# Last expert's rows in an array of their own, the other gathers beside its products, second bias added to the rows

## What is computed

```
logits = xt @ router_w + router_b
top_logit, top_idx = lax.top_k(logits, 4)          # of 32 experts
top_gate = softmax(top_logit)
for each expert e and each of its tokens:
    hid = xb @ w1[e] + b1[e]                       # 1024 -> 2048
    glu = minimum(hid[:, :1024], 7); lin = clip(hid[:, 1024:], -7, 7)
    act = glu * sigmoid(1.702 * glu) * (lin + 1)
    y   = (act @ w2[e] + b2[e]) * gate             # 1024 -> 1024
out[token] = sum of the token's four rows y
x = x + gate2 * out
```

## Time and profile before

| | |
|---|---|
| median of three runs | 2637.34 us (2634.68 to 2642.07) |
| profiled execution | 2637.1 us, span 2635.1 us, mean granted clock of TensorE 0.969 |
| PE busy | 2499.3 us (95%) |
| DVE, ACT, POOL busy | 39%, 15%, 7% |
| expert loop | about 629 to 1656 us of the span |
| end of the pass | about 1656 to 1707 us of the span |
| the chain that ended last, by engine | PE 92%, DVE 3%, ACT 2%, DMA 2%, POOL 1% |

### The profile page before, as it was taken

The page is one execution under the profiler, slowest core; times in us unless marked ns, Lnnn a source line. Parts: engine busy times, 40 slices in busy tenths (PEclk is TensorE's granted clock), DMA queues, the critical chain, the costliest instruction groups (busy, mean ns, idle before and its releaser), DMA issues.

```text
span 2635.1 us, 49056 instructions
## 1 busy us (share of the span) xinstructions
PE 2499.3 (95%) x20546; PEld 1392.9 (53%) x20546; DVE 1017.1 (39%) x2008; ACT 405.9 (15%) x797; POOL 195.1 (7%) x256
## 2 busy tenths in 40 slices
PE   5999989796999999999999999699999998999999
PEld 2444787653344433333344434345556544888888
DVE  5563655414333333333333333523145222455551
ACT  2411134412000000000000000101234201111100
POOL 0000000000111111111111111400000000000000
PEclk9999999887999999999999999799999999999999
DMA  7432000106999999999999999740200112222221
GB/s 275 156 128 96 2 3 1 67 0 248 413 422 422 421 422 422 421 422 422 422 422 422 422 422 384 253 164 33 96 33 33 32 32 64 64 96 64 88 66 54
DMA packets 143742, 555.43 MB, mean 211 GB/s; under 512 B 15760, under 2 KB 51632, under 8 KB 94240
## 3 DMA queue, kind: packets, MB, share of 16 engines
q1 hardware_dynamic: 127088, 515.22, 49.2%
q0 software_dynamic: 13984, 36.49, 3.8%
q10 hardware_dynamic: 2576, 2.36, 0.3%
HBM read 537.25 MB, written 16.78 MB: 210 GB/s over the span
## 4 chain that ended last, share of the span: by engine, by line
PE 92%; DVE 3%; ACT 2%; DMA 2%; issue 1%; POOL 1%; SPq 0%; POOLq 0%; DVEq 0%; ACTq 0%
PE psum L2501 25%; PE psum L2090 20%; PE psum L2517 13%; PE psum L2787 10%; PE psum L2816 5%; PE psum L2250 2%; PE psum L2706 2%; PE psum L2422 2%; PE psum L2683 1%; DMA ring<-in_ada_w 1%; PE psum L2364 1%; PE psum L2661 1%; PE psum L2390 1%; PE psum L2671 1%; PE psum L2078 1%
## 5 line engine op out<-in xcount | busy, mean ns | idle before, releaser
L2501 PE MATMUL psum<-ring,arena 128*32 128x512 f32 x6144 | 667.8, 594 | 10.2 <-DVE arena L1688 6.8
L2501 PEld LDWEIGHTS psum<-ring,arena 128*32 128x32 f32 x6144 | 196.8, 110 | 453.0 <-issue 452.3
L2090 PE MATMUL psum<-hT,ring 128*128 128x512 f32 x752 | 340.6, 610 | 3.5 <-ACT hT L833 3.5
L2517 PE MATMUL psum<-ring,arena 128*32 128x256 f32 x6144 | 338.3, 379 | 2.2 <-DVE arena L1722 2.1
L2517 PEld LDWEIGHTS psum<-ring,arena 128*32 128x32 f32 x6144 | 201.2, 110 | 146.5 <-issue 21.9
L2090 PEld LDWEIGHTS psum<-hT,ring 128*128 128x128 f32 x752 | 144.9, 196 | 182.2 <-issue 180.3
L1688 DVE STREAM_TRANSPOSE arena<-arena 128x768 f32<-128x768 f32 x33 | 32.3, 979 | 512.6 <-PE psum L2501 512.6
L764 POOL DMA_INDIRECT arena<-h_rows,small x102 | 99.9, 980 | 1294.8 <-issue 680.7
L2787 PE MATMUL psum<-ring 128*128 128x256 f32 x704 | 159.1, 379 | 0.5 <-ACT arena L819 0.5
L1017 ACT ACTIVATE arena<-arena 128x768 f32<-128x768 f32 x32 | 27.0, 843 | 823.3 <-DVE arena L1708 823.3
L2787 PEld LDWEIGHTS psum<-ring 128*128 128x128 f32 x704 | 133.7, 190 | 19.0 <-ACT arena L819 0.9
(11 more groups left out here) (393 smaller groups left out, 2553.3 us busy)
## 6 DMA issues: line engine op xcount, KB each, us to landing
ring<-in_exp_w SPq DMA_DIRECT2D x384, 1024.0 KB, 15.8
ring<-in_w_in SPq DMA_DIRECT2D x15, 2048.0 KB, 8.3
ring<-in_ada_w SPq DMA_DIRECT2D x12, 2048.0 KB, 7.8
ring<-in_w_ffn_in SPq DMA_DIRECT2D x22, 1024.0 KB, 7.7
expert_rows<-arena POOLq DMA_DIRECT2D x128, 96.0 KB, 6.0
ring<-in_w_ffn_out SPq DMA_DIRECT2D x8, 1408.0 KB, 6.8
ring<-in_w_out SPq DMA_DIRECT2D x2, 2048.0 KB, 7.9
ring<-in_w_o SPq DMA_DIRECT2D x2, 2048.0 KB, 8.5
```

What stands on the lines that cost most here:

```text
L2090: ins = mm(dst, l, r, start=(i == 0), stop=(i == len(parts) - 1))
L2501: ins = mm(bank[s][q * SG:(q + 1) * SG, :], XG[:, k, s * SG:(s + 1) * SG], w[:, q], start=(k == 0), stop=(k == KD - 1))
L2517: ins = mm(bank[3 + s // 2][q * SG:(q + 1) * SG, (s % 2) * 256:(s % 2 + 1) * 256], aT2k[:, s, k // 2, k % 2, :], w2_slot(k)[:, q * 256:(q ...
```

## The change

- `expert_rows` holds 31 experts; the rows of expert 31 (`LATE`) go to an HBM array of their own, `late_rows`.
- The loop has 29 rounds; two more are written out after it for PE and DVE, without number_slots and gathers for experts that do not exist (before, the loop ran these for experts 32 and 33).
- POOL stores expert 30, then issues the gathers of token tiles 0 and 1 (`fetch`), sends expert 31's rows, and issues tile 2 (after tile 0 is summed), tile 3, and after tile 2 is summed four gathers from `late_rows`, one per tile.
- The row index of each choice is clipped to the 31 experts and its gate is zeroed where the choice is expert 31 (two more small DVE steps); the gate of the late rows is taken from `GATE`.
- PE adds the four sums, then the four late tiles, so 8 rounds of 16 matmuls in place of 4.
- b2 is loaded per expert by ACT (`load_b2`, four DMAs of 1 KB), spread together with b1, and added where Y is copied out of PSUM. The load of all b2, the transposes of the gates, `GATE_T` and the L2538 products are gone.

```diff
-    keys += [("pos", t) for t in range(NT)] + [("cnt",), ("gateT",)]
+    keys += [("pos", t) for t in range(NT)] + [("cnt",)]
...
-        YR = [A(i, 2) for i in (14, 16, 18, 20, 0, 2, 4, 6, 8, 10, 12, 22, 24, 30, 14, 16)]
+        yr_room = [A(14, 2), A(16, 2), A(18, 2), A(20, 2), A(24, 2), A(30, 2), hflat[:, 4 * T:6 * T], hflat[:, 6 * T:8 * T]]
+        YR = yr_room + yr_room[1:4] + [A(0, 2), A(2, 2), A(4, 2), A(6, 2), A(8, 2)]
+        TOTAL = YR[::TOP_K]
+        YR_LATE = [yr_room[5], yr_room[6], yr_room[7], yr_room[2]]
...
-            sp.wait_ge(lin_ready, 1)
-            sp.dma_start(B2, a["exp_b2"][0]).then_inc(moe_in, 16)
...
+            def fetch(t):
+                for i in range(t * TOP_K, t * TOP_K + TOP_K):
+                    pool.indirect_dma_start(YR[i], None, y_d, ...choice_row[:, i:i + 1]...).then_inc(yr_in[t], 16)
...
-                with pool.Fori(0, EXPERTS - 1) as e:
+                with pool.Fori(0, EXPERTS - 3) as e:
                     gather(j, e + 3)
                     store(j, e)
-                store(j, EXPERTS - 1)
+                store(j, EXPERTS - 3)
+                store(j, EXPERTS - 2)
                 pool.wait_ge(rows_ready, j + 1)
                 pool.sem_inc(pool_turn, 1)
-                for i in range(NT * TOP_K):
...
+                fetch(0)
+                fetch(1)
+                send(j, LATE, y_late.rearrange("(s i) n -> s i n", s=GROUPS))
+                pool.wait_ge(choice_chain, summed(j, TOP_K))
+                pool.wait_ge(gx_sb, j * TURNS + (EXPERTS + 1))
+                fetch(2)
+                pool.wait_ge(aT_sb, j * EXPERTS + (EXPERTS + 1))
+                pool.wait_ge(w1_free, (j * EXPERTS + EXPERTS) * (QT4 * KD) + QT4 * KD)
+                fetch(3)
+                sent(j, LATE)
+                pool.wait_ge(choice_chain, summed(j, 3 * TOP_K))
+                for t in range(NT):
+                    pool.indirect_dma_start(YR_LATE[t], None, y_late, ...late_row[:, t:t + 1]...).then_inc(yr_last[t], 16)
...
+            def load_b2(e):
+                for q in range(QT4):
+                    act.dma_start(BIAS_ROWS[q * SG:q * SG + 1, 512:BIAS_N], a["exp_b2"][0][...]).then_inc(bias_in, 16)
...
-                dve.tensor_copy(Y, psum[:, 3 * T:3 * T + GROUPS * 256]...)
+                dve.tensor_tensor(Y, psum[:, 3 * T:3 * T + GROUPS * 256]..., B2[:, None, :].to_broadcast([P, GROUPS, 256]), ALU.add)
...
+                bias_arrived(j, EXPERTS - 1)
+                dve.tensor_copy(late_row, late_at).then_inc(choice_chain, 1)
+                spread_bias()
+                activations(j, LATE)
+                take_rows(j, LATE - 1)
+                turn_activations(j, LATE)
+                dve.wait_ge(bias_in, (j * EXPERTS + EXPERTS) * (32 * QT4))
+                dve.tensor_tensor(late_gate, late_gate, GATE[:, :, LATE], ALU.mult)
+                dve.stream_shuffle(BIAS_ALL, BIAS_ROWS, [0] * SG).then_inc(choice_chain, 1)
+                take_rows(j, LATE)
+                for t in range(NT):
+                    sum_rows(t)
+                for t in range(NT):
+                    dve.wait_ge(yr_last[t], j * 16 + 16)
+                    dve.tensor_scalar(YR_LATE[t], YR_LATE[t], late_gate[:, t:t + 1], None, ALU.mult).then_inc(sum_ready, 1)
...
-                for m in range(KD):
-                    mm(bank[m][:, :], B2[:, m * P:(m + 1) * P], GATE_T, start=True, stop=True)
+                for t in range(NT):
+                    pe.wait_ge(choice_chain, summed(j, (t + 1) * TOP_K))
+                    for m in range(KD):
+                        mm(bank[m][:, t * P:(t + 1) * P], TOTAL[t][:, m * P:(m + 1) * P], ident, start=(t == 0), stop=False, ...)
                 for t in range(NT):
                     pe.wait_ge(sum_ready, j * NT + (t + 1))
                     for m in range(KD):
-                        ins = mm(bank[m][:, t * P:(t + 1) * P], total[:, m * P:(m + 1) * P], ident, start=False, stop=True, ...)
+                        ins = mm(bank[m][:, t * P:(t + 1) * P], YR_LATE[t][:, m * P:(m + 1) * P], ident, start=False, stop=True, ...)
```

More of the change, by code:

```diff
@@ L334, in program @@
             "rows_ready", "mix_mm", "sum_ready", "choice_chain", "passed"))
-        yr_in = [sem(f"yr_in{t}") for t in range(NT - 1)]
-        yr_last = [sem(f"yr_last{r}") for r in range(TOP_K)]
+        yr_in = [sem(f"yr_in{t}") for t in range(NT)]
+        yr_last = [sem(f"yr_last{t}") for t in range(NT)]
         square2 = A(0, KD).rearrange("p (k t) -> p k t", k=KD)
@@ L461, in program @@
         choice_row = small[:, 16:32].bitcast(U32)
+        late_at = small[:, 96:100]
+        late_gate = small[:, 104:108]
+        late_row = small[:, 112:116].bitcast(U32)
         w1_slot = lambda k: ring[:, k * 2 * FF:(k + 1) * 2 * FF]
@@ L703, in _ @@
             w_o = a["w_o_2"][0].rearrange("(k p) n -> p k n", p=P)
-            for r in range(TOP_K):
-                sp.wait_ge(yr_last[r], passes * 16)
+            for t in range(NT):
+                sp.wait_ge(yr_last[t], passes * 16)
             for name, _ in chunks2:
@@ L767, in gather, with send @@
                 pool.sem_inc(idx_used, 1)
-            def store(j, e):
+            def send(j, e, rows):
                 pool.wait_ge(ye_sb, j * EXPERTS + (e + 2))
@@ L1769, in _ @@
                     look_up(j, e + 3)
[L1770 to L1775 removed]
+                bias_arrived(j, EXPERTS - 2)
+                turn_rows(j, EXPERTS - 1)
+                spread_bias()
+                activations(j, EXPERTS - 2)
+                take_rows(j, EXPERTS - 3)
+                turn_activations(j, EXPERTS - 2)
@@ L1782, in _ @@
                         else:
-                            dve.wait_ge(choice_chain, j * CHOICE_LINKS + (8 + t * (TOP_K - 1) + r))
-                            ins = dve.scalar_tensor_tensor(out=total, in0=YR[t * TOP_K + r], scalar=gate, in1=total,
-                                                           op0=ALU.mult, op1=ALU.add)
-                        ins.then_inc(choice_chain if r < TOP_K - 1 else sum_ready, 1)
+                            dve.wait_ge(choice_chain, summed(j, t * TOP_K + r))
```

112 lines of the change are left out of this document (62 added, 50 removed).

## The result

Over 20 runs each, the changed kernel took 2643.98 us and the kernel before 2636.75 us (medians): ratio 1.0023, 95% interval [1.0016, 1.003]. It is slower, by 7.2 us between the medians and 6.1 us by the ratio. That is less than the 0.3% that I had said a measurement can tell from no change, but the interval of these 20 runs leaves 1 out, so that limit was set too wide. (One run of 3057.83 us, at a granted clock of 0.82, is left out of the ratio.) The time forecast was 2640.1, in a range of 2633.0 to 2647.0. So the call and the range held, but the excess was put at +2.8 us and is more than twice that. And one of the prediction's own signs of being wrong has come: from the first w1 product (at 644.95, and 645.38 before) to the copy of expert 31 (1664.85, and 1655.49 before) it is 1019.9 us where it was 1010.1, 9.8 us longer, and the sign was set at 1 us.

A forecast was written before the change was run, and what follows sets the result against it. PE bounds the expert loop, with weight DMAs close behind; a chain of store, gathers and sums bounds the pass end. Last PE tile 1696.7 against 1693.9 gives +2.8 us: 2639.9, 2640.1 against the median; range 2633 to 2647.

The forecast's parts named there:

- 0.3% that I had said a measurement can tell from no change: Whole kernel: a measurement was said to tell about 0.3%, 7.9 us, from no change.
- one of the prediction's own signs of being wrong: Expert loop, first w1 product to copy of expert 31: prediction wrong if longer than before by over 1 us.
- b2 by expert: Expert loop: added small b2 loads make 1.9 us by the 30th round, below the cover, so they cost 0.
- 4.3 us of cover: Expert loop, last w1 loads: weights land in 24.7 us and may take up to 29.0 before PE waits.
- the rival of late weights: Expert loop: b2 packets make PE wait for w1 if above 0.14 us a round; 2647.2 us, chance 0.08.
- The rule that I had weighed and set aside: b2 loads in the loop: below 64 KB coalesce; read as a cost in latency, which nothing waits for.
- G = 1648.7: End of pass: first gather starts at 1648.7 us, 13.3 us before the old 1662.03.
- rows(31) "off the new path in any case": After the loop: expert 31's w2 product was said not to lie on the new path; loop exit taken as 0.
- late code: First unrolled product after the loop: 11.53 us against 10.54 inside, read as code arriving late, once; ends 0 and +1.0.
- Landing, three times in a row: End of pass: tile 0, tile 2 and late gathers each land in about 6.2 us, three waits where there were two.
- The rest of the path: End of pass, after G: tile 3 summed G + 36.7, late rows scaled G + 39.8, last PE tile ends G + 48.0.
- Edits at 0: Removed gate transposes and L2538 products, and leaving the loop two rounds earlier: each taken as 0.

The follow-up runs named there:

- e8: Changed kernel with each expert's b2 in one load of four rows instead of four 1 KB loads; ratio 1.0006 to the kernel before.
- e10: e8 plus own rooms for the late rows, gathered between tiles 2 and 3, PE taking tile 3 last; ratio 0.9999 to the kernel before.
- e2: Changed kernel with the last two w2 products as two rounds of a small loop instead of two code copies; ratio 1.0018 to the kernel before.
- e3: Changed kernel with the gathers of tiles 0 and 1 issued after expert 31's rows are sent; ratio 1.0038 to the kernel before.
- e5: Changed kernel without b2 loads in the loop, expert 0's b2 used for all (output differs); ratio 1.0007 to the kernel before.
- e12: e9 with the next part's weight loads held back until tile 3's rows have landed; ratio 1.0013 to the kernel before.
- e9: e8 plus own rooms for the late rows, stored between gathers of tiles 0 and 1, gathered after tile 1, tile 3 last on PE; ratio 1.0022.
- e1: Changed kernel with b2 loads written as sixteen pieces, which did not reach the queue, so a repeat of it; ratio 1.0022 to the kernel before.

## Why the prediction was right, and where its sizes were off

By its own steps, for the changed kernel and for e8, which is the same with the weights on time (times from the first gather, G; the stage's start is taken out where the loop is concerned):

- **b2 by expert, 0.** This is the term that was mis-sized, and the one that mattered. I priced the loads by the share of b1's packets, 0.06 us a round, and got 1.9 us of 4.3 us of cover. The landing grew by 28.0 - 23.8 = 4.2 us over the 29 rounds to 1550 us, 0.15 us a round, just over the 0.14 from which the rival of late weights decides. So the rival came true in small: expert 30's product began 989.1 us into the stage (1632.85 - 643.77) against 986.8 before. Its own price of 0.38 us a round, from POOL's packets, was too high. It also counted 64 packets a round for b2 as for b1, where the trace has 8. My error was the mean: a share over sixteen engines hides that the loads sit on one, by all that the increments and packets show, and each slot waits for its slowest engine. The Trainium skill, DMA: Bandwidth & Descriptors, section Why a DMA increments its semaphore by 16 and not by 1, says that a DMA uses the largest number of engines up to sixteen that divides the slowest dimension of both its access patterns, and that software can split a contiguous row of one partition so that it is spread. This case's trace agrees: one data packet for a load of b2, whose row is not split, eight for a load of b1, which is written as eight pieces, four for e8's load of four rows. The rule that I had weighed and set aside, in the section Rules for kernel authors of the same page of the Trainium skill, to coalesce many small transfers, pointed the right way (e8: landing 24.1), though the loss was in throughput and not in the latency that I read in it.
- **G = 1648.7.** It was 1652.67. On the stage's clock I had 1648.7 - 644.1 = 1004.6; the changed kernel has 1008.9, e8 1005.2 and e10 1005.1. With the weights on time the step was good to 0.6 us; the rest is 2.9 us by which expert 30's copy is late (999.8 us into the stage, 996.9 in e8) and 0.7 us more from its store to the first gather (7.5 against 6.8).
- **rows(31) "off the new path in any case".** Wrong as a rule: the copy of expert 31 stands ahead of tile 0's sum on DVE. It did no harm in e8 (copy at G + 4.3), and 3.0 us in the changed kernel (G + 12.2, sum at G + 13.05 instead of G + 10.06). That the product itself could slow down was no part of my sum. Its 11.53 us before I had read as late code; e2 speaks against late code. Three gathers of `h_rows` were issued beside it then, which the changed kernel and all its variants no longer have; the product takes 10.57 us in e3, e5 and e8 to e12, but these differ from before in other ways too, so this is not shown to be the reason.
- **Landing, three times in a row.** The row's 6.2 us held where the tile sums wait (6.1 to 6.2 in the changed kernel), and tile 0 was summed from G + 9.8 in e8. The first late gather was faster: 1689.56 - 1684.90 = 4.66 us to its scaling in e8, and it landed in 4.5 us after. The 3.2 us by the formula of the Trainium skill (DMA: Bandwidth & Descriptors, section Anatomy of one DMA), an estimate, were reached by no indirect gather of `expert_rows` or `late_rows` (shortest 4.1, in e2). The 6.3 us that the prediction saved by this formula start from the median 5.3; from the 6.2 of its own sum they would be 9.0.
- **The rest of the path.** In e8, tile 2's fourth gather came at G + 19.6 (forecast 20.7), its sum ended at G + 30.1 (31.6), tile 3's at G + 35.4 (36.7), the first late scaling at G + 36.3 (39.8), and the last PE tile at G + 44.7 (48.0). I had been 3.3 us too careful. In the changed kernel these 3.3 us were eaten by the late copy, and G + 48.7 looks like a good forecast for the wrong reason. That the measured time stays in the range is owed in part to this luck.
- **The sum.** For e8: +0.6 - 3.3 on the forecast +2.8 gives +0.1, which is what its stage shows (1048.4 against 1048.3), closer than two executions agree. The change itself, with b2 in one load, is worth nothing that can be measured (ratio 1.0006, from 0.9996 to 1.0016): 13 us of earlier gathers are paid back by the third landing and four more PE tiles, as forecast. For the changed kernel: 2.8 + 4.0 (G) + 0.7 (the path) = +7.5.
- **Edits at 0.** Gate transposes, leaving the loop early, the L2538 products: with b2 in one load the loop and G are where they were, so none shows a price.

## What to carry to other kernels

Where a DMA stream is close to its consumer's limit, price added loads on the one engine that they sit on, not by their mean share of sixteen: four loads of 1 KB every 31.6 us used up 4.3 us of cover in some 29 rounds, and one load of the same 4 KB, in four rows, used next to none of it (landing 24.1 for 23.8). When an event is moved forward by overlap, look at everything that it releases (e9: the next part's weights, beside gathers that still ran). And compare a stage by its own start and end: these executions entered it up to 6 us apart.

## What the runs showed of the hardware that I had not expected

- The last of a weight slot's sixteen semaphore increments fell 5.6 us behind the fifteenth over the loop (1.5 us before); the landing shows only the sum, the increments show that it is one of sixteen.
- With four small loads a round and indirect gathers beside it, the last product of 128x256 matmuls took 19.4 us from its start to the copy of its result; without the loads (e5), or without the gathers (e3), 10.8. In e1 all its matmuls had run at full pace, and PE's last four semaphore increments came 6.0 to 7.4 us after the start of their matmuls. What the loads and the gathers share isn't known.
- After about the same 2 us of idle time the granted clock was 0.50 in five kernels and 1.00 in nine, each with and without weights waited for.
